# First inputs on a queue of their own, shared last keys in the stick-breaking heads, a 512-column last projection and a last normalisation on three engines

## The reference, cut to what matters

```python
z = h @ w_in                                   # layer 1: 2048 -> 4 * 2048
q, k, v, gate = jnp.split(z, ..., axis=-1)
# stick-breaking, 16 heads of 128; for a block of queries:
z = einsum('bqhd,bshd->bhqs', qblk, kk)        # q scaled by 128 ** -0.5
visible = (pos >= 0) & (pos < qpos)            # strictly causal
sp = where(visible, softplus(z), 0)
tail[t, s] = sum of sp[t, s..t-1]
w = exp(where(visible, z - tail, -inf))
o = einsum('bhqs,bshd->bqhd', w, vv)
y = (o * silu(gate)) @ w_out                   # 2048 -> 2048
h = layer_norm(alpha * h + y, g, b)            # over the 2048 features
return h[:, 16:]                               # 256 tokens
```

## Time and profile before

| what | value |
|---|---|
| device time, median of 3 runs | 924.02 us (922.43 to 925.79) |
| the profiled execution's own device time | 926.7 us |
| its span, first to last instruction | 924.5 us |
| PE busy | 905.7 us (98%), 7594 matmuls |
| DVE busy | 548.7 us (59%) |
| ACT busy | 429.1 us (46%) |
| mean granted PE clock | 0.994 |
| DMA | 153.04 MB, mean 166 GB/s |

### The profile page before, as it was taken

The page is one execution under the profiler, slowest core; times in us unless marked ns, Lnnn a source line. Parts: engine busy times, 40 slices in busy tenths (PEclk is TensorE's granted clock), DMA queues, the critical chain, the costliest instruction groups (busy, mean ns, idle before and its releaser), DMA issues.

```text
span 924.5 us, 18765 instructions
## 1 busy us (share of the span) xinstructions
PE 905.7 (98%) x7594; PEld 890.5 (96%) x7594; DVE 548.7 (59%) x715; ACT 429.1 (46%) x672; POOL 64.0 (7%) x85
## 2 busy tenths in 40 slices
PE   8999999999999999999899999999999999999995
PEld 8999999999999999999899999999999999999995
DVE  6477667766765766765646364554646455455556
ACT  6456455645644433384444343534343444453320
POOL 1322033203200000000000000000000000000000
PEclk9999999999999999999999999999999999999998
DMA  9674465447433554224543434444343544464422
GB/s 345 223 228 163 152 219 154 135 148 219 144 121 135 186 181 172 102 93 182 187 178 137 178 139 164 154 143 174 136 181 136 181 146 167 140 227 176 186 95 91
DMA packets 25106, 153.04 MB, mean 166 GB/s; under 512 B 3392, under 2 KB 3920, under 8 KB 8560
## 3 DMA queue, kind: packets, MB, share of 16 engines
q1 hardware_dynamic: 21888, 142.61, 42.8%
q0 software_dynamic: 2896, 7.70, 4.1%
q10 hardware_dynamic: 288, 2.24, 0.6%
HBM read 150.35 MB, written 2.18 MB: 165 GB/s over the span
## 4 chain that ended last, share of the span: by engine, by line
PE 90%; DVE 5%; DMA 3%; issue 1%; ACT 1%; SPq 0%; DVEq 0%
PE bank L288 73%; PE bank L638 2%; DMA raw<-chunks 2%; PE bank L402 2%; PE bank L442 2%; DVE w_lo L935 1%; PE bank L514 1%; DMA h<-xT 1%; PE bank L550 1%; PE bank L309 1%; PE bank L310 1%; PE bank L311 1%; PE bank L528 1%; PE bank L578 0%; PE bank L417 0%
## 5 line engine op out<-in xcount | busy, mean ns | idle before, releaser
L288 PE MATMUL bank<-x_hi,w_hi 128*128 128x272 f32 (+1 forms) x1472 | 426.0, 289 | 3.0 <-ACT work L665 2.5
L288 PE MATMUL bank<-x_hi,w_lo 128*128 128x272 f32 (+1 forms) x1472 | 422.3, 287 | 0.0
L288 PE MATMUL bank<-x_lo,w_hi 128*128 128x272 f32 (+1 forms) x1472 | 422.3, 287 | 0.0
L935 DVE TENSOR_TENSOR w_lo<-raw,w_hi 128x2048 fp32r<-128x2048 f32 x127 | 291.9, 2306 | 205.0 <-ACT w_hi L660 204.6
L660 ACT ACTIVATE w_hi<-raw 128x2048 fp32r<-128x2048 f32 x128 | 244.3, 1911 | 203.4 <-PE bank L288 122.6
L288 PEld LDWEIGHTS bank<-x_hi,w_hi 128*128 128x128 f32 x1472 | 278.3, 189 | 4.4 <-issue 3.7
L288 PEld LDWEIGHTS bank<-x_hi,w_lo 128*128 128x128 f32 x1472 | 278.1, 189 | 0.0
L288 PEld LDWEIGHTS bank<-x_lo,w_hi 128*128 128x128 f32 x1472 | 277.7, 189 | 0.0
L288 PE MATMUL bank<-og_hi,w_hi 128*128 128x272 f32 x256 | 74.9, 293 | 0.0
L288 PE MATMUL bank<-og_hi,w_lo 128*128 128x272 f32 x256 | 74.1, 289 | 0.0
L288 PE MATMUL bank<-og_lo,w_hi 128*128 128x272 f32 x256 | 73.7, 288 | 0.0
(11 more groups left out here) (216 smaller groups left out, 1099.2 us busy)
## 6 DMA issues: line engine op xcount, KB each, us to landing
raw<-chunks SPq DMA_DIRECT2D x128, 1024.0 KB, 4.8
work<-bias_table POOLq DMA_DIRECT2D x8, 512.0 KB, 5.7
work<-chunks SPq DMA_DIRECT2D x4, 512.0 KB, 11.8
work<-bias_table POOLq DMA_DIRECT2D x8, 256.0 KB, 6.5
work<-ln_rows ACTq DMA_DIRECT2D x1, 2048.0 KB, 7.2
out<-work SPq DMA_DIRECT2D x8, 256.0 KB, 2.3
h<-xT SPq DMA_DIRECT2D x3, 544.0 KB, 9.2
raw<-chunks SPq DMA_DIRECT2D x4, 256.0 KB, 4.7
```

The costliest lines, as they stand in the source:

```text
L288: last = mm(o, l, r, start=(kt == 0 and n == 0), stop=(kt == KT - 1 and n == 2))
L935: V.tensor_tensor(w_lo[:, slot, :, :], raw[:, half, :, :], w_hi[:, slot, :, :].bitcast(f32), ALU.subtract).then_inc(lo_ready, 1)
```

## The change

1. **Start.** `X_EARLY` goes from 1 to 4: ACT issues the first four pieces of `xT`, SP starts with the weights. Tiles 4-7 of `xT` come as two pieces (4-5 and 6-7), and `term_by_term` covers tiles 0 to 5. `SPINS_0` goes from 14 to 16.
2. **Stick-breaking heads.** The keys' last 16 of both heads stand side by side in one block of 128 (`B_ENDS`), so one matmul, one mask and one transpose serve both heads. Head 0 has 400 columns and head 1 has 432. The two masks of a head's own columns are one matmul. Values turned for both heads go to one bank and are copied out by one 512-column and one 128-column ACT instruction. Both heads' outputs lie in one bank, and `pv_done` rises by 2 at its end.
3. **Last projection.** `RW = 512`: four slices of 512 columns instead of eight of 256. A piece is now a quarter of the features of a 512-column slice, and each slice has its own two banks. The last slice for u = 1 stays as two groups of 256 columns.
4. **Last rows.** Of the last 128 tokens, columns 1024 to 2047 are normalised by DVE as before. For columns 0 to 1023 DVE multiplies the rows by the gain ahead of time, PE adds the gain times the negative mean and the offset times the standard deviation (a matmul over two rows of statistics), and ACT multiplies by the inverse root on the way out.

```diff
-        X_PARTS = ((0, 1), (1, 2), (2, 3), (3, 4), (4, 8), (8, 12), (12, 16))
-        X_A, X_EARLY = len(X_PARTS), 1
+        X_PARTS = ((0, 1), (1, 2), (2, 3), (3, 4), (4, 6), (6, 8), (8, 12), (12, 16))
+        X_A, X_EARLY = len(X_PARTS), 4
...
-            for k in range(4):
+            for k in range(6):
                 term_by_term(k)
-            for k in range(4, HALF):
+            for k in range(6, HALF):
...
                     mm(z[:, 0:B_K1], k[:, 0:128], q, start=True, stop=False)
                     mm(z[:, B_K1:B_K2], k[:, 128:256], q[:, B_Q1:SEQ], start=False, stop=False)
-                    mm(z[:, B_K2:B_Z], k[:, T - 128:T], q[:, B_Q2:SEQ], start=False, stop=False)
-                    mm(z[:, 0:B_Q1], ident_r[:], mask_r[:, 0:B_Q1], start=False, stop=False)
-                    mm(z[:, B_K1:B_Z], ident_r[:], mask_r[:, 128:128 + B_Z - B_K1], start=False, stop=True) \
-                        .then_inc(z_ready, 1)
+                    m = mm(both(z[:, 0:128], B_K1), ident_r[:], mask_r[:, 0:256].rearrange("p (a b) -> p a b", b=128),
+                           start=False, stop=(u == 0))
+                    if u == 0:
+                        m.then_inc(z_ready, 1)
+                z = z_bank[1][:, B_K2:B_K2 + B_L]
+                mm(z, b["kT"][:, B_ENDS], b["q"][:, :, B_Q2:SEQ], start=False, stop=False)
+                mm(z, ident_r[:], mask_r[:, 256:256 + B_L], start=False, stop=True).then_inc(z_ready, 1)
...
-                    nc.tensor.transpose(o[:, 256:384], v[:, T - 128:T], ident[:]).then_inc(vtb_ready, 1)
+                m.then_inc(vtb_ready, 1)
+                nc.tensor.transpose(bank[5][:, 0:128], b["vT"][:, B_ENDS], ident[:]).then_inc(vtb_ready, 1)
...
+                last = b["w"][:, B_LAST].rearrange("p (a c) -> p a c", c=META)
+                mm(o_b[:, :, B_Q2:SEQ], b["V_last"], last, start=False, stop=True).then_inc(pv_done, 2)
...
+            for j in range(ROW_ITERS - 1):
+                if j == 1:
+                    pe.wait_ge(r_ready, 8)
+                for c in range(4):
+                    quarter_arrived(j, c)
+                    for u in range(2):
+                        if j == 0 and c == 0:
+                            pe.wait_ge(tile_free[u], P_OUT_B)
+                        last = row_quarter(row_acc[j][u], u, c, slice(0, RW))
...
+            for c in range(4):
+                quarter_arrived(ROW_ITERS - 1, c)
+                last = row_quarter(row_acc[ROW_ITERS - 1][0], 0, c, slice(0, RW))
...
+            for c in range(2):
+                pe.wait_ge(r_scaled, c + 1)
+                mm(bank[2 + c][:], ident[:], scaled_r[:, c * 512:(c + 1) * 512], start=True, stop=False)
+            pe.wait_ge(stats_ready, 2)
+            nc.tensor.transpose(acc[0][0:2, 0:128], stats, ident[:]).then_inc(stats_turned, 1)
+            for c in range(2):
+                mm(bank[2 + c][:], stats_row, row_gb[:, c * 512:(c + 1) * 512], start=False, stop=True) \
+                    .then_inc(sums_ready, 1)
...
+            for j in range(ROW_ITERS - 1):
+                for c in range(4):
+                    act.wait_ge(raw_loaded[c % 2], 16 * (P_OUT_B + 2 * j + c // 2 + 1))
+                    act.wait_ge(*((quarter_used, 3 * j + c + 1) if c < 3 else (tile_full[1], P_OUT_B + j + 1)))
+                    A(w_hi[:, c, :, :], raw[:, c % 2, :, :], ACT.Copy).then_inc(hi_ready, 1)
...
+            for c in range(2):
+                act.wait_ge(sums_ready, c + 1)
+                A(f["r"][:, 1, c * 512:(c + 1) * 512], bank[2 + c][:], ACT.Identity, scale=bn_mv[:, 1, 2:3]) \
+                    .then_inc(act_out, 1)
...
-            normalise_tokens(1, range(4))
+            normalise_tokens(1, range(2, 4))
```

More of the change, by code:

```diff
@@ L240, in _, with store @@
                     load(RAW_SLOTS * r + s, s)
[L242 to L246, removed]
+            def store(j, c, ready, count):
+                sp.wait_ge(ready, count)
+                sp.dma_start(out[j * 128:(j + 1) * 128, c * 512:(c + 1) * 512],
+                             f["r"][:, j, c * 512:(c + 1) * 512]).then_inc(stored, 16)
+            for c in range(4):
+                store(0, c, out_ready, c + 1)
+            store(1, 2, out_ready, 5)
+            store(1, 0, act_out, 1)
+            store(1, 3, out_ready, 6)
+            store(1, 1, act_out, 2)
             sp.wait_ge(stored, 16 * 8)
@@ L320, in term_by_term @@
                          for c, o in enumerate((acc, v_acc)) for u in range(2)]
[L321 removed]
+                part = [k in range(*cut) for cut in X_PARTS].index(True)
+                pe.wait_ge(x_hi_ready, part + 1)
                 if k == 0:
@@ new lines, in row_quarter @@
+            def row_quarter(o, u, c, cols):
+                for k in range(QUARTER):
+                    kt = QUARTER * c + k
+                    whi, wlo = (w[:, c].rearrange("p a b -> p (a b)")[:, k * RW + cols.start:k * RW + cols.stop]
+                                for w in (w_hi, w_lo))
+                    part = slice(u * 128, u * 128 + 128)
+                    terms = ((og_hi, whi), (og_lo, whi), (og_hi, wlo))
+                    for n, (m, w) in enumerate(terms):
+                        last = mm(o[:, 0:cols.stop - cols.start], m[:, kt, part], w,
+                                  start=(kt == 0 and n == 0), stop=(kt == KT - 1 and n == 2))
+                return last
@@ L868, in body_b @@
                     split_hi(P + 4, 0)
-                parts = [(z_bank[u][:, 0:B_Z], b["w"][:, u, :]) for u in range(2)]
+                parts = [(z_bank[u][:, 0:c.stop - c.start], b["w"][:, c]) for u, c in enumerate(B_HEADS)]
                 act.wait_ge(pv_done, PV_A + 2 * i)
@@ L1234, in body_b @@
                     split_lo(P + p, half)
-                parts = [(z_bank[u][:, 0:B_Z], b["w"][:, u, :], b["sp"][:, u, :]) for u in range(2)]
+                parts = [(z_bank[u][:, 0:c.stop - c.start], b["w"][:, c], b["sp"][:, c]) for u, c in enumerate(B_HEADS)]
                 dve.wait_ge(pt_copied, PT_A + 2 * i)
@@ L1468 @@
                    np.stack([halves[0][1], halves[1][1]])]
-    chunks = np.stack(halves).reshape(N_CHUNKS, 128, HALF * CW)
+    rows = [w_ob[:, i * RW:(i + 1) * RW].reshape(4, QUARTER, 128, RW).transpose(0, 2, 1, 3) for i in range(ROW_ITERS)]
+    chunks = np.concatenate([v.reshape(-1, 128, HALF * CW) for v in halves + rows])
     d_loc, d_all = 255 - np.arange(LOC), T - 1 - np.arange(T)
```

184 lines of the change are left out of this document (109 added, 75 removed).

## The result

The changed kernel takes 913.38 us (median of 4 runs, 911.95 to 916.56) against 923.42 us (4 runs, 922.43 to 925.79) for the kernel before: ratio 0.9886, 95% interval 0.9865 to 0.9907. That is 10 us faster, where 9.2 was forecast. The profiled execution took 913.77 us with a span of 911.9 us, so 12.6 us less span than before; some 2.7 us of that turn out to be no work of the change.

What follows compares the result with a forecast made beforehand. The prediction took PE, busy 98% of the span, to bound the kernel. Its terms, 1.7 + 4.1 + 1.8 + 1.6 = 9.2 us, took the median from 924.0 to 914.8, given as 915.0 us, range 910.5 to 919.

Steps and rivals of the forecast that it cites:

- the likeliest case: Whole kernel: the prediction's own forecast, a time of 912.5 to 917 us, chance 0.64.
- 1. start: Start: tile 4 begins at about 12.1 us instead of 14.17, saving 1.7 us; bounds 0.5 and 2.3 us.
- 2. heads: Stick-breaking heads: 0.55 us saved in each of seven passes and 0.25 us in pass 0, 4.1 us in the sum.
- 3. projection: Last projection: 512-column matmuls 0.231 us apart, saving 1.8 us; bounds 0 and 7.8 us.
- 4. end: After PE's last projection matmul: last rows shared by DVE, PE and ACT, 1.6 us gained; bounds 0 and 2.3 us.
- Some comes back: Start: weights' low part for tiles 8 to 11 ready at 18.56 us, PE asks at about 18.2; 2.0 us becomes 1.7.
- an earlier issue can fill a little: Start: load rate was only 183 GB/s between 2 and 4 us, so issuing earlier gains a little; 1.7 us, not 1.6.
- rival of a fixed cost: Last projection: overhead is fixed per matmul, so 512 columns cost 0.225 us and 3.9 us is saved, 912.9 us; chance 0.12.
- Sums ready at +4.5 and +5.3, stored columns at +5.1 and +5.95: End: times in us after PE's last projection matmul for PE's two 512-column sums and ACT's scaled columns.
- a sign of being wrong: End: the prediction is wrong if ACT's last scaling ends after DVE's by more than 1 us.
- 0, if PE runs these matmuls at 1.2 GHz: End: lower bound of the gain, 0 us, if PE's clock is low or a hand-over is slow.
- The change leaves it as it is: Second pass of body_b: PE's 2.5 us wait and the low clock behind it, some 1.7 us, are not altered.

Runs made afterwards that it cites:

- x_no_start: Changed kernel with the start of the kernel before (one input piece from ACT, tiles 4 to 7 as one piece, 14 spins): 915.53 us, ratio 0.9925.
- x_no_heads: Changed kernel with the stick-breaking heads as before (416 columns each, own product, masks, transpose and output bank for the last keys): 917.51 us, ratio 0.9937.
- x_narrow: Changed kernel with each 512-column product of the last projection made as two of 256 columns: 915.64 us, ratio 0.9914.
- x_no_tail: Changed kernel with the last rows normalised by DVE alone, as before: 914.54 us, ratio 0.9911.
- x_one_queue: Changed kernel with only the first input tile issued by ACT (X_EARLY = 1), new pieces and term-by-term order kept: 913.95 us, ratio 0.9907.
- x_whole_piece: Changed kernel with input tiles 4 to 7 as one piece and term by term only for tiles 0 to 3, X_EARLY = 4 kept: 915.38 us, ratio 0.9902.
- x_changed: The changed kernel itself, run again beside three of its variants: 913.48 us, ratio 0.9892 to the kernel before.
- x_tail_spin: Changed kernel with 9 idle PE matmuls before the statistics' transpose in the end and 3 behind it: 912.93 us, ratio 0.9887.
- x_query_first: Changed kernel, but in the stick-breaking loop passes ACT empties the query's two banks before splitting the next projection's weights: 911.7 us, ratio 0.987.
- x_combined: Changed kernel with the query emptied first, only the first input tile issued by ACT, and idle PE matmuls around the statistics' transpose: 912.3 us, ratio 0.9881.

## Why the prediction came out right, and where its terms were off

The time (915.0 forecast, 913.4 measured) lies in the likeliest case, 912.5 to 917. That it lies so close is in part luck: the heads gave more than forecast and the end less, and the two nearly cancel. Of the 1.6 us that are left, 0.6 come from the median of the kernel before, 923.4 now for 924.0 then. By its own parts, with the forecast, what traces give, and what medians give:

| part | forecast | traces | medians |
|---|---|---|---|
| 1. start | 1.7 | 1.9 at 299 us | 2.1 (x_no_start) |
| 2. heads | 4.1 | 4.9 | 4.0 (x_no_heads) |
| 3. projection | 1.8 | 1.73; 1.56 for the width alone | 2.2 (x_narrow) |
| 4. end | 1.6 | 0.6 to 1.3 | 1.1 (x_no_tail) |
| sum | 9.2 | 9.0 to 9.8 | 9.4; 10.0 measured at once |

**Start.** Right in mechanism and size: tile 4 at 11.92 us for the "about 12.1" of the text. "Some comes back" was right as well, but not where it was put: tile 8 was not late, and 0.4 us came back by 299 us, with the wait of 0.59 us at 75 us. The sentence that an earlier issue can fill a little did not hold for the small pieces: x_one_queue has the table as early. The Trainium skill, "DMA: Bandwidth & Descriptors", section "Issuing engines are not separate DMA queues", has it that a second issuer saves only issue time. The runs agree, with the bias table at 30.03 us from one queue and 30.09 from two. But with the large piece the issue time was 1.4 us (2.75 us against 4.2), and that took most of PE's wait away in x_whole_piece; the prediction, which went by the size of the piece, did not weigh this.

**Heads.** The mechanism was right, the size per pass too small: 0.70 us for 0.55. Start to start in the traces, `scores_b` went from 2.211 to 1.844 us (0.37 for 0.30), the transposes and tails gave 0.11 as forecast, and `attend_b` went from 1.715 to 1.492 (0.22 for 0.14). PE's timeline of `attend_b` in the kernel before:

```profile
604.08 0.59 PE L550 MATMUL bank<-work 128*128 128x256 f32 x2
604.51 0.41 PE L551 MATMUL bank<-work 128*128 128x144 f32 x2
604.76 0.29 PE L552 MATMUL bank<-work 128*128 128x16 f32 x2
604.90 0.68 PE L550 MATMUL bank<-work 128*128 128x256 f32 x2
605.41 0.41 PE L551 MATMUL bank<-work 128*128 128x144 f32 x2
605.66 0.29 PE L552 MATMUL bank<-work 128*128 128x16 f32 x2
605.80 0.36 PE L288 MATMUL bank<-x_hi,w_hi 128*128 128x256 f32 x1
```

and after:

```profile
596.90 0.59 PE L581 MATMUL bank<-work 128*128 128x256 f32 x2
597.33 0.41 PE L582 MATMUL bank<-work 128*128 128x144 f32 x2
597.57 0.59 PE L581 MATMUL bank<-work 128*128 128x256 f32 x2
598.00 0.41 PE L582 MATMUL bank<-work 128*128 128x144 f32 x2
598.25 0.30 PE L584 MATMUL bank<-work 128*128 128x32 f32 x2
```

The same product of 256 columns takes 604.51 - 604.08 = 0.43 us behind long matmuls but 605.41 - 604.90 = 0.51 us behind the one of 16 columns; after the change both take 0.43. That is the missing 0.08. The weight loads in the same traces fit: the load for this product begins at 604.87 us in the kernel before, 0.03 us ahead of the product, and at 597.45 after the change, 0.12 us ahead. My reading is that the weights come late behind so short a matmul; no run tested it by itself. I had counted a removed instruction by its own distance to the next alone. In the scores the neighbour gives 0.04 (0.47 against 0.43 us in the same place), and the wide mask costs less than I charged for it. In pass 0 almost nothing came through, where 0.25 us was forecast: between the scores of passes 0 and 1 x_no_heads and x_changed, with waits of 0.38 and 0.45 us, take 53.94 and 53.86 us.

**Projection.** Right: 0.232 us for 0.231, no wait among the 384, 1.73 us for 1.8. With this the rival of a fixed cost (0.225 us) falls. The rule that the prediction took from the Trainium skill, "TensorE: Matmul & The Clock Gate", section "Back-to-back issue gap", gives 216 ns where the trace has 232. The prediction left out that the page calls this the gap of an isolated matmul; its figure for a stream, about 131 ns for 512 columns, is still further off.

**End.** The step that was off is the hand-over to PE. "Sums ready at +4.5 and +5.3, stored columns at +5.1 and +5.95": in the profiled execution ACT ended at +5.9 and +7.6 instead, because the later steps of L707 took 0.853 us each for the 0.44 taken. That is 2.3 us after DVE's end, and the prediction had named over 1 us as a sign of being wrong. At full clock (x_one_queue, x_tail_spin) the second ends at +6.2 and +6.1, 0.9 and 0.8 us after DVE's, and the last store is issued at +6.3 and +6.2, where +6.1 was forecast. The bound "0, if PE runs these matmuls at 1.2 GHz" was too harsh: even then 0.6 us is left. With the clock held the end is 9.65 us, forecast 9.2. Most of the rest is in the stores: with four of them issued within 1.5 us, the span ends 3.4 us after the last issue in x_tail_spin (906.9 to 910.3), 2.9 before (921.6 to 924.5), so 0.5 us more, where I had allowed 0.2.

**The second pass.** "The change leaves it as it is" fits the medians: the same edit gave 1.7 us on both kernels (923.5 to 921.9, 913.4 to 911.7), so as far as they tell the wait has no part in the 10 us. For a single execution it does not hold: "PE still waiting at the second pass, 2.5 to 3 us" was forecast, and it was 1.42. But it has a part in the profiled 12.6: the wait was 2.47 us before and 1.42 after, and 3.4 us at half speed behind the first had none behind the second, some 2.7 us together, by chance. Over ten traces of kernels with the old order it was 0.2 to 2.5 us; the load that ACT waits for lands now earlier, now later. In two of the ten, at 2.47 and 2.19 us, the clock fell behind it; in x_narrow, at 2.49 us, it did not. It is a part of the scatter of the times, how large a part isn't shown: x_query_first spreads over 0.9 us in its 4 runs and the changed kernel over 4.6 in 4, but x_combined, with the new order too, over 2.9 in 5. The kernel before spreads over 5.3 us in 17 runs, and over 3.5 in 12 with the edit.

The fastest kernel here is x_query_first, 911.7 us. Its interval touches that of the changed kernel, so for the pair alone the gain isn't proven; for the edit on the kernel before it is.

## What to carry to other kernels

Take the cost of a small matmul from where the next same instruction starts with and without it in front, not from its own distance: a very short one makes its neighbour dearer. On an engine that serves two masters in order (here ACT, which splits weights and empties banks), put the work that another engine waits for ahead of the work that waits for a DMA; it cost 0.03 us a pass here and removed a wait that comes and goes by chance. A wider matmul that was already long saves little (0.004 us per pair here, 1.56 us over 336 pairs); count it by its distance in the trace. And before a gain between two profiled executions is put down to the change, look at which waits differ that the change doesn't touch.

## What the runs showed of the hardware

- The distance of fp32r matmuls at 2.4 GHz grows faster than their columns: medians of 0.118 us for 256, 0.127 for 272 and 0.232 for 512, which are 0.012, 0.014 and 0.019 us above columns / 2.4 GHz. The few of 416 columns in `tails` took 0.187 to 0.195 us in a stream, and 0.27 behind a product of 32 columns.
- After PE's last projection matmul it had 1.88 us of work, 1.11 us idle, one short transpose and 0.45 us idle in each of the eight traces with the split end and no idle matmuls, and yet the clock fell at different times, 3.9 to 7.0 us after the last addition. The four products begin at 3.5 us and at 2.4 GHz end at 5.5, with 0.43 us from one to the next; at 1.2 GHz it is 0.853; the end was 10.30 us with the earliest fall, 9.91 with the next and 9.65 to 9.73 in the other six. With the first gap filled the products ran at 2.4 GHz in both traces (x_tail_spin, x_combined).
- A piece split at the place where two engines wait for it, together with the new order of PE's work there, was worth about 2 us at the start. A second issuing engine gave nothing on top of it, but with the large piece it had tile 4's low parts ready 0.7 to 2.2 us earlier (one trace against three).
